# Two-layer trunk with eight experts on one core: order of work at six places of the kernel

## The chip, the cores and the metric

The kernel runs on one core of one Trainium2 chip. The core has TensorE (matrix products, PE in the profile), VectorE (DVE), ScalarE (ACT), GpSimd (POOL) and SyncE (SP), each with a queue of its own that it works through in order; engines wait for each other by semaphores. The metric is the device time of one execution in microseconds (us).

## The reference, cut to what matters

```python
SEQ, D_MODEL = 256, 1024
h = x
# layer 0: one input projection, MLA attention (8 heads) and band attention (8 heads, with a
# learned relative bias), output projection, then a dense SwiGLU
u = rmsnorm(h, g) @ ev_w_in                       # 1024 x 1952
h = h + concat(mla(u), band(u, rel_bias)) @ ev_w_out
h = h + (silu(rmsnorm(h) @ gate) * (rmsnorm(h) @ up)) @ down      # hidden 2752
# layer 1: differential attention, output projection, then top-2-of-8 expert SwiGLU
q, k, v = split(rmsnorm(h) @ od_w_qkv)            # 1024 x 3072
h = h + diff_attention(q, k, v) @ od_w_out
t = rmsnorm(h)
combine = top2_softmax(t @ router)                # 256 x 8
for e in range(8):
    h = h + combine[:, e:e+1] * swiglu(t, gate[e], up[e], down[e])    # hidden 3584
```

## The kernel before

All products are made in three passes to keep float32 accuracy: each weight and each activation is split into a high part (`w_hi`, `xT_hi`, written by ScalarE) and a low rest (`w_lo`, `xT_lo`, written by VectorE), and `product` (L1626) runs hi by hi, hi by low and low by hi. Weights come in units of 1 MB (128 x 2048 floats) in the order of `weight_stream` and, for each expert, `expert_stream` (42 units: gate, up and down of seven chunks of 512 hidden columns, down one chunk behind). A unit goes from memory to `raw` (4, later 7 slots), ScalarE makes `w_hi` and VectorE `w_lo` in a ring of three slots (`SPLIT`), TensorE uses it and counts `unit_used`. So ScalarE can start a unit only when the unit three before it has been used (L625, L860), and `split_to(end)` makes an engine work off the units up to `end` at that place of its queue.

The start: x is transposed by quarters (128 tokens by 512 columns; `norm_turn`), scaled by the gain (`norm_scale`), split (`norm_part` on ScalarE, `norm_low` on VectorE) and used by `project`; the norm's root is applied when the projection is read. The relative bias table is loaded to `rel` by ScalarE's queue (L602), extended by VectorE (L1131), stored to `rel_scratch` by POOL (L2056), waited for, and read back in eight shifted copies (L2060, `bias_rev`); VectorE adds the mask to them (L1190) after router_g and before its part of the second, third and fourth weight units and of the first projection's copy (L1192).

The output projections (`out_projection`) take four units of two k blocks each. The last one goes through `last_unit` (L1644), which works bank by bank (four PSUM banks, tokens by halves of the columns), so that VectorE's residual adds (`add_quarter`, L1049) and TensorE's transposes for the next norm can follow. `add_and_norm` (L1051) is VectorE's order there; ScalarE's is at L771 to L780 (units, table load, norm parts), for the odd layer at L923 to L940.

The dense feed-forward loops over six chunks of 512 (the last of 192): gate and up of chunk j, with the transposes of the hidden product of chunk j-1 into bank 3 behind the gate units (L1848), then the down units of chunk j-1. The last chunk's down unit goes through `last_unit` again.

Routing, ahead of the experts: logits, top 2 (L1437), rank of each token in its expert, gate values (`gates`), and a list of up to three spare items for experts with more than 128 tokens (`spare_items`), all in small VectorE operations; `select` writes 0/1 matrices and TensorE gathers the tokens of two experts at a time. At an expert's end y is read from banks 6 and 7 by ScalarE and VectorE (`outputs`), scattered by TensorE (`scatter`) during the next expert's first units, and added to h (`add_scattered`). After the last expert h goes out in two stores of 128 tokens (L559).

## Time and profile before

| | us |
|---|---|
| median of 3 runs | 1510.41 |
| lowest, highest run | 1499.75, 1512.85 |
| profiled execution, device time | 1512.85 |
| its span, first to last instruction | 1510.7 |

The profile is of one execution. Times in its rows are us from the span's start. A timeline row has the start, the duration, the engine, the line of the kernel, the operation with its tiles, how often it ran in a row, and in brackets how long the engine had been idle and what released it. A queue name with a q (SPq, ACTq) is the issue of a DMA. PEclk is the TensorE clock that was granted, 1.00 being 2.4 GHz and 0.50 being 1.2 GHz.

### The profile page before, as it was taken

To read this page: it belongs to the slowest core of one execution; us is meant where nothing else is said; L and a number is where in the kernel's file an instruction comes from. 1 tells how busy PE (TensorE), PEld (TensorE's weight loads), DVE (VectorE), ACT (ScalarE), POOL (GpSimd) and SP (SyncE) were. 2 spreads that over 40 slices of the span, in tenths; PEclk is the share of its full clock that TensorE was granted. 3 is DMA by queue.
4 is the path that set the end of the run, shared out by engine and by line. 5 is a ranking of instruction groups with operands and counts; after the bars stand their busy time and mean duration, and the time that the engine had idled before them with its cause. 6 is when DMAs were issued, how large, how long until landed. Compare 5 with 4: busy or idle time off the path is not lost.

```text
span 1510.7 us, 17809 instructions
## 1 busy us (share of the span) xinstructions
PE 1448.6 (96%) x6624; PEld 1194.1 (79%) x6624; DVE 1180.3 (78%) x1003; ACT 957.8 (63%) x833; POOL 8.4 (1%) x49
## 2 busy tenths in 40 slices
PE   7989999999987899999999999999999999999997
PEld 5768788886866778888888888888888888888886
DVE  6873554445687688898889889988889988888986
ACT  4562544343464567777777777777777776777774
POOL 2000000000000000000000000000000000000000
PEclk9976999997997899999999999999999999999999
DMA  7400855364532289999999999999999999999992
GB/s 259 162 0 29 307 194 187 111 212 138 170 109 70 98 315 372 375 344 377 379 311 380 371 353 370 378 335 342 372 372 351 377 377 311 371 378 353 367 379 103
DMA packets 181294, 421.51 MB, mean 279 GB/s; under 512 B 9192, under 2 KB 12316, under 8 KB 181212
## 3 DMA queue, kind: packets, MB, share of 16 engines
...
q10 hardware_dynamic: 2496, 0.23, 0.1%
q14 instruction: 25, 0.20, 0.0%
HBM read 419.28 MB, written 1.06 MB: 278 GB/s over the span
## 4 chain that ended last, share of the span: by engine, by line
PE 84%; DVE 10%; ACT 3%; issue 2%; DMA 1%; ACTq 0%; SPq 0%; DVEq 0%
PE ps L1628 25%; PE ps L1630 25%; PE ps L1629 25%; DVE w_lo L1004 2%; PE ps L1959 2%; DVE w_lo L1404 2%; PE ps L1926 1%; DVE h L1525 1%; ACT w_hi L627 1%; PE ps L1711 1%; PE ps L1704 1%; DVE work L1110 1%; DMA raw<-in_ev_w_in_dram 1%; PE ps L1703 1%; PE ps L1641 1%
## 5 line engine op out<-in xcount | busy, mean ns | idle before, releaser
L1404 DVE TENSOR_TENSOR w_lo<-raw,w_hi 128x2048 fp32r<-128x2048 f32 x336 | 768.7, 2290 | 110.3 <-ACT w_hi L861 109.5
L861 ACT ACTIVATE w_hi<-raw 128x2048 fp32r<-128x2048 f32 x336 | 644.2, 1919 | 246.0 <-PE ps L1630 246.0
L1628 PE MATMUL ps<-w_hi,xT_hi 128*128 128x512 f32 (+2 forms) x1312 | 517.9, 395 | 16.3 <-DVE w_lo L999 4.8
L1630 PE MATMUL ps<-w_hi,xT_lo 128*128 128x512 f32 (+2 forms) x1312 | 510.3, 389 | 0.0
L1629 PE MATMUL ps<-w_lo,xT_hi 128*128 128x512 f32 (+2 forms) x1312 | 509.8, 389 | 0.0
L1628 PEld LDWEIGHTS ps<-w_hi,xT_hi 128*128 128x128 f32 x1312 | 248.8, 190 | 68.7 <-issue 11.9
L1630 PEld LDWEIGHTS ps<-w_hi,xT_lo 128*128 128x128 f32 x1312 | 248.6, 189 | 51.4
L1629 PEld LDWEIGHTS ps<-w_lo,xT_hi 128*128 128x128 f32 x1312 | 249.1, 190 | 48.0
L1004 DVE TENSOR_TENSOR w_lo<-raw,w_hi 128x2048 fp32r<-128x2048 f32 (+4 forms) x65 | 138.4, 2138 | 109.8 <-ACT w_hi L627 109.6
L1628 PE MATMUL ps<-w_hi,hT_hi 128*128 128x512 f32 (+1 forms) x548 | 217.8, 397 | 3.0 <-DVE hT_lo L1018 1.9
L1630 PE MATMUL ps<-w_hi,hT_lo 128*128 128x512 f32 (+1 forms) x548 | 215.6, 394 | 0.0
L1629 PE MATMUL ps<-w_lo,hT_hi 128*128 128x512 f32 (+1 forms) x548 | 215.3, 393 | 0.0
L627 ACT ACTIVATE w_hi<-raw 128x2048 fp32r<-128x2048 f32 (+4 forms) x65 | 115.7, 1790 | 130.5 <-PE ps L1630 130.5
L1628 PEld LDWEIGHTS ps<-w_hi,hT_hi 128*128 128x128 f32 (+1 forms) x548 | 104.3, 190 | 27.7 <-issue 3.9
L1630 PEld LDWEIGHTS ps<-w_hi,hT_lo 128*128 128x128 f32 (+1 forms) x548 | 104.4, 191 | 22.0
L1629 PEld LDWEIGHTS ps<-w_lo,hT_hi 128*128 128x128 f32 (+1 forms) x548 | 104.6, 191 | 20.5
L886 ACT ACTIVATE hT_hi<-ps 128x512 fp32r<-128x512 f32 x56 | 33.2, 592 | 9.8 <-PE ps L1959 9.8
L1531 DVE TENSOR_TENSOR hT_lo<-ps,hT_hi 128x512 fp32r<-128x512 f32 x56 | 38.3, 684 | 1.3 <-ACT hT_hi L886 1.3
L1547 DVE TENSOR_TENSOR prod_e<-sil_e,ps 128x512 f32<-128x512 f32 x56 | 38.1, 680 | 0.4 <-PE ps L1630 0.4
L1959 PEld LDWEIGHTS ps<-ident,prod_e 128*128 128x128 f32 x224 | 27.1, 139 | 11.7 <-DVE h L1525 2.9
L1959 PE MATMUL ps<-ident,prod_e 128*128 128x128 f32 x224 | 33.8, 273 | 2.5 <-DVE h L1525 2.5
L1711 PE MATMUL ps<-ident,work 128*128 128x128 f32 x72 | 19.6, 404 | 14.5 <-DVE work L1364 11.4
...
## 6 DMA issues: line engine op xcount, KB each, us to landing
...
```

Source lines behind the costliest of these rows:

```text
L627: ins = act.activation(w_hi[0:r, n % SPLIT, a:a + m], raw[0:r, raw_of(n), a:a + m], ACT.Copy)
L861: act.activation(w_hi[:, (DENSE + q) % SPLIT, :], raw[:, r, :], ACT.Copy).then_inc(hi_ready, 1)
L886: act.activation(hT_hi[:, :, side(m)], blocks(4 + m % 2), ACT.Copy).then_inc(hT_part, 1)
L1004: ins = dve.tensor_tensor(w_lo[0:r, n % SPLIT, a:a + m], raw[0:r, raw_of(n), a:a + m], w_hi[0:r, n % SPLIT, a:a + m].bitcast(F32), ALU.sub ...
L1404: dve.tensor_tensor(w_lo[:, k, :], raw[:, raw_of(DENSE + q), :], w_hi[:, k, :].bitcast(F32), ALU.subtract).then_inc(lo_ready, 1)
L1531: dve.tensor_tensor(hT_lo[:, :, side(m)], blocks(4 + m % 2), hT_hi[:, :, side(m)].bitcast(F32), ALU.subtract).then_inc(hT_ready, 1)
L1547: dve.tensor_tensor(prod_e[:, j % 2, :], sil_e[:, j % 2, :], ps[:, 2 * (j % 2) + 1, :], ALU.mult).then_inc(prod_done, 1)
L1628: pe.matmul(out, x_hi, hi, start=start, stop=False)
L1629: pe.matmul(out, x_hi, lo, start=False, stop=False)
L1630: return pe.matmul(out, x_lo, hi, start=False, stop=stop)
L1711: ins = pe.transpose(ps[:, 2 + head % 2, n * P:(n + 1) * P], s[:, slot, n * P:(n + 1) * P], ident[:, :])
L1959: ins = pe.transpose(ps[:, 4 + j % 2, n * P:(n + 1) * P], prod_e[:, j % 2, n * P:(n + 1) * P], ident[:, :])
```

## The change

Start: weight unit 0 is loaded in two halves with a semaphore each, TensorE begins with its first half (`first_unit`), the order of norm parts and half units on ScalarE and VectorE is changed (`first_low`), the other gains are loaded behind unit 2, and the loads of positions and `rel` are issued behind the fourth norm part, with the extension of `rel` behind `norm_reciprocals(0)` on VectorE. Output projections: units 2 and 3 go through `last_two`, bank by bank over four k blocks, and are both released at its end; VectorE leaves one unit to be split for later (also at the last down unit, where `split_to(last_down + SPLIT)` becomes `split_to(last_down + SPLIT - 1)`) and takes it up inside `add_and_norm`. Feed-forward: the two halves of the last chunk are transposed after the first down unit of chunk 4, the second one into bank `LAST_BANK` (0); VectorE's rest for hT_lo reads the same bank. Routing: `low_tokens(0)` goes behind `select`, the gathers of the high parts come first, ScalarE takes one of the two low copies and loads the table for Silu early; `gates` and the spare items go into the units of expert 0, with the prefix sum over eight counts in three doubling steps instead of seven. Expert's end: the last down unit finishes bank 6 before bank 7, ScalarE and VectorE read them one by one, scatter and adds go by column halves, and h is stored in four parts.

The diff, cut; declarations, the bodies of the small routing functions and VectorE's side of the bank change are left out.

```diff
@@ -508,7 +514,12 @@
     for n in range(DENSE):
-        if n == 2:
+        if n == 0:
+            for c, done in enumerate((first_landed, landed[0])):
+                dst = raw[:, 0, c * UNIT // 2:(c + 1) * UNIT // 2].rearrange("p (k n) -> p k n", k=2)
+                sp.dma_start(dst, w_in[:, 2 * c:2 * c + 2, 0:N]).then_inc(done, 16)
+            continue
+        if n == 3:
@@ -553,11 +564,13 @@
     spare(0)
-    for t in range(TT):
-
-        sp.wait_ge(scatter_read, 4 * (n_over + E) - 2 * (TT - 1 - t))
-        sp.dma_start(out[0, t * P:(t + 1) * P, :], h[:, t, :]).then_inc(stored, 16)
-    sp.wait_ge(stored, 16 * TT)
+    for n in range(4):
...
+        sp.wait_ge(scatter_read, 4 * (n_over + E) - (3 - n))
+        sp.dma_start(out[0, t * P:(t + 1) * P, v], h[:, t, v]).then_inc(stored, 16)
+    sp.wait_ge(stored, 16 * 4)
@@ -598,8 +611,6 @@
     act.dma_start(gain_rows[G_MIX0:G_MIX0 + DC, :], w["ev_norm_mix"][0].rearrange("(k p) -> k p", p=P)).then_inc(mix_landed, 16)
-    act.dma_start(pos_i[:, :], w["positions"][0].rearrange("(t p) -> p t", p=P)).then_inc(pos_landed, 16)
-    act.dma_start(rel[:, 0:2 * B_CLIP + 1], w["ev_b_rel_bias"][0]).then_inc(rel_landed, 16)
@@ -616,11 +627,13 @@
         for n in range(done[0], min(end, DENSE)):
-            act.wait_ge(landed[raw_of(n)], 16 * landings(n))
             if n == 0:
+                act.wait_ge(first_landed, 16)
                 act.activation(w_hi[:, 0, 0:UNIT // 2], raw[:, 0, 0:UNIT // 2], ACT.Copy).then_inc(first_hi, 1)
+                act.wait_ge(landed[0], 16)
...
                 continue
+            act.wait_ge(landed[raw_of(n)], 16 * landings(n))
@@ -703,9 +716,12 @@
     norm_part(0, 0)
+    norm_part(0, 1)
     split_to(1)
-    for f in range(1, 4):
-        norm_part(0, f)
+    norm_part(0, 2)
+    norm_part(0, 3)
+    act.dma_start(pos_i[:, :], w["positions"][0].rearrange("(t p) -> p t", p=P)).then_inc(pos_landed, 16)
+    act.dma_start(rel[:, 0:2 * B_CLIP + 1], w["ev_b_rel_bias"][0]).then_inc(rel_landed, 16)
@@ -786,10 +802,11 @@
                 whole, s = m // P, TT * (j - 1) + t
+                bank = LAST_BANK if j == FCH and t == 1 else 3
...
                 if m % P:
-                    act.activation(hT_hi[0:m % P, whole, t * P:(t + 1) * P], ps[0:m % P, 3, whole * P:(whole + 1) * P], ACT.Copy)
-                act.activation(hT_hi[:, 0:whole, t * P:(t + 1) * P], blocks(3, whole), ACT.Copy).then_inc(ff_hT_hi, 1)
+                    act.activation(hT_hi[0:m % P, whole, t * P:(t + 1) * P], ps[0:m % P, bank, whole * P:(whole + 1) * P], ACT.Copy)
+                act.activation(hT_hi[:, 0:whole, t * P:(t + 1) * P], blocks(bank, whole), ACT.Copy).then_inc(ff_hT_hi, 1)
@@ -876,8 +893,10 @@
     def outputs(i):
-        act.wait_ge(unit_used, i * len(EXPERT) + (DENSE + len(EXPERT)))
+        act.wait_ge(y_psum, i + 1)
         for nn in range(2):
+            if nn:
+                act.wait_ge(unit_used, i * len(EXPERT) + (DENSE + len(EXPERT)))
@@ -940,14 +959,19 @@
     for half in range(2):
-        act.wait_ge(gather_psum, 2 * half + 1)
+        act.wait_ge(gather_psum, half + 1)
...
                        ACT.Copy).then_inc(x_hi_ready, 1)
+    act.wait_ge(gather_psum, 4)
+    bank = FIRST_BANK[3]
+    act.wait_ge(x_lo_ready, 1)
+    act.activation(xT_lo[:, 4:8, :], ps[:, bank:bank + 2, :].rearrange("p b (c n) -> p (b c) n", n=T), ACT.Copy).then_inc(x_lo_ready, 1)
...
     ins.then_inc(gate_exp, 1)
+    act.activation(unread[:, :], eps[:, :], ACT.Silu)
@@ -1058,8 +1083,9 @@
         norm_low(c, 1)
+        norm_low(c, 2)
+        split_to(last + SPLIT)
         norm_scale(k, first, c, 3)
-        norm_low(c, 2)
@@ -1127,24 +1153,24 @@
             ins.then_inc(yT_ready, 1)
-    dve.wait_ge(rel_landed, 16)
-    dve.tensor_copy(rel[:, 2 * B_CLIP + 1:384],
-                    rel[:, 2 * B_CLIP:2 * B_CLIP + 1].to_broadcast([B_HEADS, 383 - 2 * B_CLIP])).then_inc(rel_extended, 1)
...
     norm_low(0, 0)
-    split_to(1)
+    first_low(0, first_hi, first_lo)
     norm_low(0, 1)
+    first_low(1, hi_ready, lo_ready)
...
     norm_reciprocals(0)
+    dve.wait_ge(rel_landed, 16)
+    dve.tensor_copy(rel[:, 2 * B_CLIP + 1:384],
+                    rel[:, 2 * B_CLIP:2 * B_CLIP + 1].to_broadcast([B_HEADS, 383 - 2 * B_CLIP])).then_inc(rel_extended, 1)
@@ -1295,7 +1321,7 @@
     low_y(0, 1)
-    split_to(WIDE_FROM + 2)
+    split_to(WIDE_FROM + 1)
@@ -1404,8 +1431,7 @@
                           ALU.subtract).then_inc(lo_ready, 1)
-    for q in range(SPLIT - 1):
-        split_unit(0, q)
+    split_unit(0, 0)
@@ -1453,7 +1479,6 @@
     link(dve.tensor_scalar(g[:, 9, :, :], g[:, 6, :, :], -FAR, FAR, ALU.mult, ALU.add))
-    low_tokens(0)
@@ -1467,33 +1492,43 @@
-    def spare_items():
...
-        for e in range(1, E):
-            link(dve.tensor_tensor(load8[:, 1, e:e + 1], load8[:, 1, e - 1:e], load8[:, 0, e - 1:e], ALU.add))
...
+    def spare_counts():
...
+    def spare_picks():
...
         link(ins)
...
+    def spare_item(s):
...
+        pick = load8[:, 2 + s:3 + s, :].to_broadcast([P, TT, E])
...
+        dve.tensor_tensor(load8[:, 5 + s, :], load8[:, 2 + s, :], slots_f[:, 0:E], ALU.mult)
...
+    def spare_list():
@@ -1541,6 +1576,17 @@
         for q, (kind, j, u) in enumerate(EXPERT):
+            if routing:
+                if q == 4:
+                    gates()
+                if q == 10:
+                    spare_counts()
+                if q == 16:
+                    spare_picks()
+                if q in (22, 28, 34):
+                    spare_item((q - 22) // 6)
+                if q == 40:
+                    spare_list()
@@ -1566,19 +1612,18 @@
     select(1, 1).then_inc(sel_ready, 1)
-    low_tokens(1)
-    for half in range(2):
-        dve.wait_ge(gather_psum, 2 * half + 2)
-        bank = FIRST_BANK[2 * half + 1]
-        dve.tensor_copy(xT_lo[:, 4 * half:4 * half + 4, :],
-                        ps[:, bank:bank + 2, :].rearrange("p b (c n) -> p (b c) n", n=T)).then_inc(x_lo_ready, 1)
+    for t in range(TT):
+        low_tokens(t)
+    dve.wait_ge(rank_psum, 2)
+    link(dve.tensor_scalar(load8[:, 0, :], ps[:, 7, 0:E], float(P), None, ALU.is_gt))
+    split_unit(0, 1)
+    dve.wait_ge(gather_psum, 3)
+    bank = FIRST_BANK[1]
+    dve.tensor_copy(xT_lo[:, 0:4, :], ps[:, bank:bank + 2, :].rearrange("p b (c n) -> p (b c) n", n=T)).then_inc(x_lo_ready, 1)
     split_unit(0, SPLIT - 1)
-    gates()
-    dve.wait_ge(rank_psum, 2)
-    spare_items()
+    expert(0, 0, False, False, True)
+    expert(1, 0, True, True)
     dve.wait_ge(routed, 1)
-    expert(0, 0, False, False)
-    expert(1, 0, True, True)
@@ -1657,10 +1702,47 @@
             norm_turn(k, f)
+    def last_two(layer, u, hi, lo, hi_2, lo_2):
...
+        for f in range(4):
+            t, half = quarter(f)
...
+            for c in range(4):
+                k = 2 * u + c
+                a, b = (hi, lo) if c < 2 else (hi_2, lo_2)
+                ins = product(ps[:, 4 + TT * t + half, :], xT_hi[:, k, tok], xT_lo[:, k, tok], a[:, c % 2, col], b[:, c % 2, col],
+                              False, c == 3)
+            if f < 3:
+                ins.then_inc(out_psum, 1)
+            else:
+                ins.then_inc(unit_used, 2)
+            if 1 <= f:
+                norm_turn(2 * layer + 1, f - 1)
+        norm_turn(2 * layer + 1, 3)
...
+    def first_unit():
...
+        for c in range(4):
+            if c == 0:
+                pe.wait_ge(first_lo, 1)
+            if c == 2:
+                pe.wait_ge(lo_ready, 1)
+            for t in range(TT):
+                if c == 0:
+                    pe.wait_ge(xT_ready, t + 1)
...
+                ins = product(ps[:, 4 + t, :], xT_hi[:, c, tok], xT_lo[:, c, tok], w_hi[:, 0, col], w_lo[:, 0, col], c == 0, False)
+        ins.then_inc(unit_used, 1)
...
             for u in range(2):
+                if layer == 0 and j == 0 and u == 0:
+                    first_unit()
+                    continue
@@ -1747,8 +1829,8 @@
             hi, lo = split(AT[f"out{layer}", 0, u])
-            if u == DC // 2 - 1:
-                last_unit(2 * layer, 2 * layer + 1, (P, P), xT_hi[:, 2 * u:2 * u + 2, :], xT_lo[:, 2 * u:2 * u + 2, :], hi, lo, True)
+            if u == DC // 2 - 2:
+                last_two(layer, u, hi, lo, *split(AT[f"out{layer}", 0, u + 1]))
@@ -1823,6 +1905,15 @@
     out_projection(0)
+    def turn_hidden(j, t, bank):
...
+        m = cols(j, FF)[1]
+        pe.wait_ge(ff_prod, TT * j + t + 1)
+        for n in range(-(-m // P)):
+            k = min(P, m - n * P)
+            ins = pe.transpose(ps[0:k, bank, n * P:(n + 1) * P], prod[:, t, n * P:n * P + k], ident[:, :])
+        ins.then_inc(ff_turned, 1)
@@ -1845,16 +1936,10 @@
                     ins.then_inc(unit_used, 1)
-                if kind == "gate" and j >= 1:
-
-                    m, s = cols(j - 1, FF)[1], TT * (j - 1) + u
-                    pe.wait_ge(ff_prod, s + 1)
-                    if s >= 1:
-                        pe.wait_ge(ff_hT, s)
...
-                    ins.then_inc(ff_turned, 1)
+                if kind == "gate" and 1 <= j < FCH:
+                    if j >= 2 or u == 1:
+                        pe.wait_ge(ff_hT, TT * (j - 1) + u)
+                    turn_hidden(j - 1, u, 3)
@@ -1872,6 +1957,10 @@
                     ins.then_inc(unit_used, 1)
+                if j == FCH - 1 and k % 4 == 1:
...
+                    turn_hidden(j, 0, 3)
+                    turn_hidden(j, 1, LAST_BANK)
@@ -1929,9 +2018,10 @@
         pe.wait_ge(selT_ready, count)
-        pe.wait_ge(y_lo_ready, 2 * i + 2)
         for n in range(4):
-            t, nn = divmod(n, 2)
+            nn, t = divmod(n, 2)
+            if t == 0:
+                pe.wait_ge(y_lo_ready, 2 * i + nn + 1)
@@ -1971,11 +2061,13 @@
             if kind == "down":
-                for c in range(2):
-                    for nn in range(2):
-                        col = slice(c * D + nn * N, c * D + (nn + 1) * N)
-                        ins = product(ps[:, 6 + nn, :], hT_hi[:, 2 * u + c, side(j)], hT_lo[:, 2 * u + c, side(j)], hi[:, col], lo[:, col],
-                                      j == 0 and u == 0 and c == 0, j == ECH - 1 and u == 1 and c == 1)
+                last = j == ECH - 1 and u == 1
+                for c, nn in ([(0, 0), (1, 0), (0, 1), (1, 1)] if last else [(0, 0), (0, 1), (1, 0), (1, 1)]):
+                    col = slice(c * D + nn * N, c * D + (nn + 1) * N)
+                    ins = product(ps[:, 6 + nn, :], hT_hi[:, 2 * u + c, side(j)], hT_lo[:, 2 * u + c, side(j)], hi[:, col], lo[:, col],
+                                  j == 0 and u == 0 and c == 0, last and c == 1)
+                    if last and (c, nn) == (1, 0):
+                        ins.then_inc(y_psum, 1)
@@ -2017,9 +2109,9 @@
     gather(0, FIRST_BANK[0], T)
+    gather(2, FIRST_BANK[2], T)
...
     gather(1, FIRST_BANK[1], T)
-    gather(2, FIRST_BANK[2], T)
```

## Rows read from the trace of the kernel before

**Rows 1.** The page's first part: busy time, share, instructions

```profile
PE 1448.6 (96%) x6624; PEld 1194.1 (79%) x6624; DVE 1180.3 (78%) x1003; ACT 957.8 (63%) x833; POOL 8.4 (1%) x49
```

**Rows 2.** Windows: PE, PEld, DVE, ACT, POOL busy; PEclk, DMA share, GB/s

```profile
166.00:330.00 164.00, 162.65 (x758) 134.29 (x756) 78.63 (x55) 67.30 (x57) 0.00 (x0) 1.00 0.56 186
1270.00:1390.00 120.00, 119.56 (x543) 98.75 (x542) 107.35 (x62) 88.23 (x60) 0.00 (x0) 1.00 1.00 366
```

**Rows 3.** Timeline (start, duration, engine, line, idle before), start of the kernel

```profile
10.14 1.06 ACT L621 ACTIVATE w_hi<-raw 128x1024 fp32r<-128x1024 f32 x1 [0.57 <-DMA raw<-in_ev_w_in_dram]
...
13.69 0.76 PE L1628 MATMUL ps<-w_hi,xT_hi 128*128 128x512 f32 x1 [4.82 <-DVE w_lo L999]
```

**Rows 4.** Timeline, DMA chain of the bias table

```profile
7.89 0.22 DVE L1131 COPY work<-work 8x127 f32<-8x127 f32 x1 [7.89 <-DMA work<-in_ev_b_rel_bias_dram]
...
15.54 4.27 POOL L2060 DMA_DIRECT2D raw<-rel_scratch  x8 [6.47 <-DMA rel_scratch<-work]
```

**Rows 5.** DMA issues of 0 to 40 us: queue, count, KB each, us to landing

```profile
raw<-rel_scratch POOLq DMA_DIRECT2D x8, 128.0 KB, 4.0
...
pos_i<-in_positions_dram ACTq DMA_DIRECT2D x1, 1.0 KB, 6.7
...
rel_scratch<-work POOLq DMA_DIRECT2D x1, 12.0 KB, 6.8
```

**Rows 6.** One line's instructions: the gain_ff load on POOL, ns each, start

```profile
L2063 POOL DMA_DIRECT2D gain_ff<-in_od_norm_ff_dram x1: 533/533/533, 487.4 to 487.4; - x1
...
DMA to landing us min/median/max: 3.9/3.9/3.9
```

**Rows 7.** Timeline, behind the bias adds

```profile
28.75 2.77 DVE L1190 TENSOR_TENSOR work<-raw,mask 128x256 f32<-128x256 f32 x8
...
33.78 0.50 PE L1628 MATMUL ps<-w_hi,xT_hi 128*128 128x512 f32 x1 [0.41 <-DVE w_lo L1004]
...
39.83 1.00 PE L1687 MATMUL ps<-ident,work 128*128 128x128 f32 x6 [0.32 <-DVE work L1201]
```

**Rows 8.** Timeline, gap in expert 0

```profile
534.07 0.50 PE L1628 MATMUL ps<-w_hi,xT_hi 128*128 128x512 f32 x1 [3.52 <-DVE w_lo L1404]
```

**Rows 9.** Windows as in rows 2: attention, last feed-forward chunk, behind the gap

```profile
85.00:133.00 48.00, 45.32 (x189) 37.82 (x189) 25.02 (x58) 25.58 (x77) 0.00 (x0) 0.56 0.07 23
...
352.00:366.00 14.00, 14.00 (x36) 8.60 (x36) 8.94 (x10) 4.79 (x7) 0.00 (x0) 0.50 0.43 150
...
536.00:538.00 2.00, 2.00 (x6) 1.52 (x6) 2.00 (x2) 0.00 (x0) 0.00 (x0) 0.50 1.02 389
```

**Rows 10.** Timeline, end of the even output projection

```profile
156.62 1.92 ACT L627 ACTIVATE w_hi<-raw 128x2048 fp32r<-128x2048 f32 x1 [3.52 <-PE ps L1630]
158.56 1.28 ACT L643 ACT_TABLE_LOAD   x1
...
161.52 0.66 PE L1641 MATMUL ps<-ident,h 128*128 128x128 f32 x4 [0.91 <-DVE h L1049]
...
165.03 0.47 PE L1628 MATMUL ps<-w_hi,xT_hi 128*128 128x512 f32 x1
```

**Rows 11.** Timeline, last feed-forward chunk

```profile
338.43 0.74 DVE L1320 SCALAR_TENSOR_TENSOR work<-ps,rstd,work 128x192 f32<-128x192 f32 x2
...
350.58 0.79 PE L1628 MATMUL ps<-w_hi,hT_hi 128*128 128x512 f32 x1 [1.04 <-DVE hT_lo L1313]
...
366.41 0.78 PE L1628 MATMUL ps<-w_hi,xT_hi 128*128 128x512 f32 x1
```

**Rows 12.** Timeline, routing

```profile
510.93 0.17 DVE L1435 COPY gate_t<-ps 128x16 f32<-128x16 f32 x1 [1.04 <-PE ps L1907]
...
516.00 2.08 PE L1926 MATMUL ps<-sel,xg_hi 128*128 128x256 f32 x8 [0.64 <-DVE sel L1503]
...
531.52 0.17 DVE L1497 CAST over_i<-over_s 128x4 int32<-128x4 f32 x1
```

**Rows 13.** Timeline, end of the kernel

```profile
1502.60 2.73 DVE L1525 SCALAR_TENSOR_TENSOR h<-ps,comb,h 128x512 f32<-128x512 f32 x4 [0.89 <-PE ps L1937]
```

71 lines of the change are left out of this document (37 added, 34 removed).

## Prediction

> **What bounds the kernel now.** I read the page first [rows 1]: TensorE is busy 1448.6 of 1510.7 us, so 62 us at most are gaps. Then I cut the span into stages [rows 2]. In the experts (busy 119.56 of 120 us, full clock) and in the feed-forward middle (162.65 of 164 us) TensorE has no gap to give back; a change can only pay there if it removes TensorE work, and this one removes none. The time that can move lies in six places: the start, the two ends of the output projections, the last feed-forward chunk, the routing ahead of expert 0, and the end. For each I read the timelines of the engines, since a wait by itself does not tell what is next in the queue. Every engine runs its queue in order, so I look for what stands behind each wait.
>
> The sum is made against the profiled execution (span 1510.7, device time 1512.85, 2.1 us around it). The median of the three runs is 1510.41, and I carry the difference over to it unchanged. The three runs themselves lie 13 us apart, so the kernel can't tell less than about 1% (15 us) from no change.
>
> **Start, first the gain.** Weight unit 0 comes in two halves, and its halves are split around the norm parts. Before, the first product starts at 13.69, released by the second half of w_lo [rows 3]. Now it needs only the first. ScalarE's first half of w_hi starts at 10.14 and takes 1.06 [rows 3]; a norm part now stands ahead of it, but that fits before 10.2, so the half is there at 11.25, and VectorE's half of w_lo, about 1.2, at 12.5. TensorE starts 1.2 us earlier.
>
> **Start, then the loss.** The load of `rel` is issued after the fourth norm part, and VectorE's extension of it now stands behind norm_reciprocals. Behind that lies a chain on POOL that the diff does not touch: store to rel_scratch, wait, eight reads into bias_rev. Before, the extension ran at 7.89, the store took 6.8 us, the reads started at 15.54, the last at 19.3, landing 4.0 us later: 15.2 us from the end of the extension (8.1) to 23.3 [rows 4, 5]. VectorE came to the bias adds at 28.75 and did not wait: 5.4 us of cover. After: the instructions ahead of the extension are the same ones and end at 20.5 in the trace of before and a few tenths later now, 20.9; `rel`, issued near 16.3, lands 4 to 6.7 us later (the 6.7 is that of pos_i beside it [rows 5]), so the extension ends at about 21.5 (20.9 to 22.5). Plus 15.2 is 36.7. The store of before ran beside the weight loads; the one POOL DMA of a quiet time, gain_ff's, took 3.9 [rows 6]. I take the store in the middle, 1.5 us shorter: 35.2 (33.2 with the short store and early extension, 37.7 with the long ones). The bias adds then wait 6.5 us (4.4 to 9.0). Behind them on VectorE stand w_lo of unit 3, which TensorE already waited for at 33.78, w_lo of unit 4, the copy of the first projection and the norms up to TensorE's transposes at 39.83 [rows 7]; all of it moves by the whole wait, and the 1.2 us gained above is swallowed by it. TensorE then stands idle some 8 us. After a gap of 3.5 us at 530 to 534 it ran at the lower level (granted 0.50, 1.2 GHz) until 538 [rows 8, 9]; the 24 products of unit 3 at 0.43 instead of 0.23 us for some 5 us end at 10.3 us after the bias adds where c_normed is ready at 8.1 (39.6, from the end of the bias adds at 31.5): 2.0 us more. Start: +8.5 (5 to 11.5).
>
> The Trainium skill ("DMA: Bandwidth & Descriptors", Anatomy of one DMA) gives a fixed part of about 2.0 us for a DMA of the gpsimd path, against 6.8 us in the row of the store. With 2.0 us for the store and some 2.3 for a read, an estimate from that page, the bias would be there at about 30, the wait 1.3 us, and the sum below 1500 to 1501. That is the second rival.
>
> **Output projections, even layer.** Units 2 and 3 are taken together, bank by bank, and both are given back at the end (unit_used by 2). Gain: VectorE no longer has w_lo of gate unit 1 (2.29) ahead of the residual adds, which cost TensorE 0.91 us at 160.6 [rows 10]. The 48 products (0.2275 each) and two turns from 150.9 end at 162.9, against 163.4. But ScalarE's queue is unchanged: w_hi of gate unit 1, which needs unit 2's slot, then the table load, then the norm parts. Before that w_hi ran at 156.62, under unit 3, and the table load behind it [rows 10]. Now it can't start before 162.9: 1.92 for w_hi, 1.48 for the table load (1.28) and its dummy, 0.63 for the norm part, 0.69 for xT_lo, with handovers 167.8. Gate's first product was at 165.03: +2.8. TensorE has then stood for 3.5 us, the size of the gap in [rows 8], whose 3.5 us at half clock cost 1.7. Even layer: +4.5 (3.7 without the clock but with a 0.9 us wait for w_lo of gate unit 1; 5.5 with a longer low stretch).
>
> **Last feed-forward chunk.** Before, both token halves of the last chunk are turned only after the last down unit of chunk 4 (347.6), with ScalarE, VectorE and bank 3 in series; TensorE starts the last unit at 350.58 and runs it and the transposes at half clock (0.50 over 352 to 366), and the qkv projection starts at 366.41 [rows 9, 11]. VectorE's products were ready at 339.2 [rows 11], so the new turns in mid-down (342) wait for nothing. Then: 347.63 + 0.6 for the moved turns + 18 products (4.1) + turn (0.55) + 6 products (1.4) + turns, the last behind an add of 0.68 and xT_lo of 0.69 = 355.7, at full clock. Gain 10.7, plus 0.4 for the tail at half clock, less 0.7 for w_lo of the second qkv unit, which VectorE reaches at 361.9 when TensorE wants it at 361.2. Feed-forward: -10.4 (-8.5 to -12).
>
> **Odd layer and routing.** Here too ScalarE's w_hi of expert unit 1 waits for the joint release: E = 505.4, w_hi to 507.3, then four copies (0.5 to 0.6) and two squares (1.2) in series: roots at 512.2, logits copied at 512.8 against 510.93. low_tokens(0) no longer stands before the rank (1.28), so the selection ends 1.45 later, not 1.9, and gathers start at 517.45 instead of 516.0 [rows 12]. xT_lo of the first half comes behind w_lo of unit 1: expert 0 starts at 524.05 instead of 522.37. Now the gain: gates and spare items (525.74 to 531.69, 5.9 us, the last of them in [rows 12]) no longer stand before w_lo of unit 3. ScalarE has two table loads and the exponentials first, so w_hi(3) ends at 530.3, w_lo(3) at 532.6, and TensorE goes on at 532.6 instead of 534.07 [rows 8]: 1.5, and I count 1.4. No gap of 3.5 us, so no low stretch: 1.7. Routing: -3.1 (-4.5 to 0).
>
> The some 45 small operations go to seven places in expert 0, about 1 us each. VectorE has 2 us free in each 16.4 us (six w_lo of 2.2, two others of 0.65), and w_lo is ready 1.2 us ahead of its unit, so I charge 0.5 in all (0 to 3).
>
> **Experts' ends.** Seven of eight are covered: the next expert's units run meanwhile, and the releasing order of banks is the same. At the last one y_hi of bank 6 starts six products (1.37 us) earlier, so the last add ends near 1503.8 instead of 1505.3 [rows 13]; four stores of half a row block instead of two, and the last one is 256 KB and does not share with 512 KB: 1.5 + 1.2. End: -2.7 (-1.4 to -3.5).
>
> **Sum.** +8.5 + 4.5 - 10.4 - 3.1 + 0.5 - 2.7 = -2.7 us: span 1508.0, and against the median 1507.7.
>
> **Rivals.** (1) The forecast: two new stalls eat the feed-forward gain; 1507.7. Chance 0.60. (2) The bias is back by 30 us, with both kinds of POOL DMA quicker than any of before; then the start costs 1 instead of 8.5: 1507.7 - 7.5 = 1500.2. For it speaks that the weight loads of the first 20 us are over, against it that even the quiet one of [rows 6] took 3.9 and that eight issues take 4.3 in series. Decides: the landing of the last bias read, before or after 30. Chance 0.20. (3) Neither the start nor the even layer stalls, and both small gains there are kept: -10.4 - 3.1 - 2.7 - 1.2 - 0.9 = 1492. Against it the order of ScalarE's queue. Chance 0.05. (4) The other side: after 8 us of idleness TensorE stays at the lower level through the rest of the input stage, as it did over most of 85 to 133 us [rows 9]; some 30 us of products between 41 and 85 us would cost 15 to 25 us more: 1523 to 1533. It decides if the low stretch lasts past 60 us. Against it: the stretch of [rows 8] ended under unbroken products, and in the input stage they are nearly unbroken. Chance 0.05. (5) The early turns do not do what they say: the last unit still waits, for w_lo or the adds, and the low clock stays; half of the 10.4 is lost: 1512.9. Chance 0.10.
>
> **Chances and range.** Faster by over 1% (below 1495.3): rival 3 and a low draw of rival 2, 0.07. Slower by over 1% (above 1525.5): rival 4 and a little of 5, 0.05. Within: 0.88. The bounds of the terms, all at one end, give 1499.1 (+5 + 3.7 - 12 - 4.5 - 3.5 = -11.3) and 1520.5 (+11.5 + 5.5 - 8.5 + 3 - 1.4 = +10.1); hardly all lean one way, so I cut the top to 1517, and take the bottom to 1495, since rival 2 lies at 1500 before its own terms vary. That holds rivals 1, 2 and 5 but for their outer ends: 8 in 10.
>
> **What would show it.** First product near 12.5; VectorE idle ahead of the bias adds, released by the DMA of bias_rev, 4 to 9 us; TensorE idle from about 32.5 with clock 0.50 behind it. ScalarE's w_hi at the end of the even projections starting with the last product, TensorE idle some 3.5 us. No ScalarE wait of 9 us before the last chunk's hT_hi and clock 1.00 there. No TensorE gap of 3.5 us in expert 0. If the bias read lands under 30 us the first term is wrong; if the w_hi starts earlier than the last product, the second.

## The result and the profile after

| | before | after |
|---|---|---|
| median of 19 runs each | 1508.20 us | 1514.21 us |
| lowest, highest run | 1485.36, 1514.14 | 1496.37, 1517.10 |
| profiled execution, device time | 1512.85 us | 1517.07 us |
| its span | 1510.7 us | 1514.9 us |
| ratio after to before | | 1.0075, 95% interval 1.0044 to 1.0106 |

The changed kernel is slower, by 6.0 us in the medians (0.4%). The ratio of 1.0075 leaves out runs that lie over 1.5% above the fastest of their kernel, the upper eleven of before's 19 and none of after's; with all 19 runs of each the means give 1.0046. The forecast was 2.7 us faster.

The two profiled executions differ by 4.2 us. I set the same points of the work beside each other, from the timelines of TensorE (us from the start):

```
point on TensorE                                     before    after   offset   step
first product of weight unit 0                        13.69    10.67    -3.02
first product of the up-projection (hT)               42.77    51.91    +9.14   start    +9.14
first transpose of the attention output              132.85   141.96    +9.11            -0.03
wait for the first gate's silu                       180.26   194.55   +14.29   even     +5.18
wait for the last gate's silu                        332.59   346.87   +14.28            -0.01
wait for the odd layer's normed q and k              433.98   438.99    +5.01   last FF  -9.27
first gather for expert 0                            516.00   523.18    +7.18   odd      +2.17
first transposes of expert 0                         543.97   546.02    +2.05   routing  -5.13
last transposes of expert 7                         1490.97  1496.52    +5.55   experts  +3.50
end of the span                                     1510.7   1514.9     +4.2    end      -1.35
```

The steps add up to +4.2. The first part of the page after, to be read against [rows 1]: TensorE is busy 3.7 us less, its gaps are 7.9 us longer.

```profile
PE 1444.9 (95%) x6624; PEld 1191.7 (79%) x6624; DVE 1177.8 (78%) x1003; ACT 959.5 (63%) x835; POOL 8.4 (1%) x49
```

Now the stages. The timeline after, start of the kernel, all engines, to be read against [rows 3, 4, 7]:

```profile
8.27 1.04 ACT L632 ACTIVATE w_hi<-raw 128x1024 fp32r<-128x1024 f32 x1
...
10.67 0.47 PE L1673 MATMUL ps<-w_hi,xT_hi 128*128 128x512 f32 x1 [2.32 <-DVE w_lo L1018]
...
21.25 0.22 DVE L1172 COPY work<-work 8x127 f32<-8x127 f32 x1 [2.32 <-DMA work<-in_ev_b_rel_bias_dram]
...
26.09 4.28 POOL L2152 DMA_DIRECT2D raw<-rel_scratch  x8 [3.65 <-DMA rel_scratch<-work]
...
36.87 2.77 DVE L1216 TENSOR_TENSOR work<-raw,mask 128x256 f32<-128x256 f32 x8 [9.14 <-DMA raw<-rel_scratch]
...
41.89 0.80 PE L1673 MATMUL ps<-w_hi,xT_hi 128*128 128x512 f32 x1 [9.58 <-DVE w_lo L1027]
```

The chain is the one foretold: extension at 21.25, store, reads, VectorE 9.14 us idle in front of the bias adds, TensorE 9.58 us idle behind it. The DMA issues of 0 to 40 us after, against [rows 5]: the store is quicker (4.0, was 6.8), the reads slower (6.2, was 4.0).

```profile
raw<-rel_scratch POOLq DMA_DIRECT2D x8, 128.0 KB, 6.2
...
rel_scratch<-work POOLq DMA_DIRECT2D x1, 12.0 KB, 4.0
```

The end of the even output projection after, timeline, against [rows 10]: ScalarE's w_hi is the last product's follower, the table load stands behind it, and gate starts 3.54 us late.

```profile
172.12 1.91 ACT L640 ACTIVATE w_hi<-raw 128x2048 fp32r<-128x2048 f32 x1 [9.95 <-PE ps L1675]
174.05 1.28 ACT L656 ACT_TABLE_LOAD   x1
...
177.01 0.76 PE L1673 MATMUL ps<-w_hi,xT_hi 128*128 128x512 f32 x1 [3.54 <-DVE xT_lo L1041]
```

Windows after (busy us of PE, PEld, DVE, ACT, POOL, then PEclk, DMA share, GB/s), behind the two new gaps, in the last feed-forward chunk and in expert 0, against [rows 9]. Behind both gaps TensorE runs at 1.2 GHz (granted 0.50, the first window already holds some full clock); in the last chunk, where before it had 0.50 over 352 to 366, it now has 1.00; and expert 0 has no gap left.

```profile
42.00:46.00 4.00, 4.00 (x11) 3.16 (x12) 3.04 (x4) 1.78 (x2) 0.00 (x0) 0.57 0.73 225
...
177.00:181.00 4.00, 3.99 (x10) 3.13 (x11) 2.64 (x5) 2.59 (x7) 0.00 (x0) 0.50 0.81 299
...
352.00:366.00 14.00, 14.00 (x62) 10.58 (x61) 7.64 (x12) 7.15 (x10) 0.00 (x0) 1.00 0.72 243
530.00:546.00 16.00, 15.93 (x70) 12.81 (x69) 11.67 (x12) 13.33 (x12) 0.00 (x0) 1.00 0.79 282
```

The qkv projection of after starts at 371.30, 4.89 us later than in [rows 11] instead of 14.3. What the forecast had not reckoned with lies in the experts. From expert to expert the first transposes are 120.4 or 120.5 us apart, with a pair's gathers 123.8 to 124.2, and at one place more: from expert 3 to expert 4, where the loop over the middle pairs jumps back, before takes 124.96 and after 128.07. The timelines of VectorE and then of TensorE at that place, before:

```profile
1008.44 1.23 DVE L1510 CAST xT_lo<-ps 128x1024 fp32r<-128x1024 f32 x1 [0.89 <-PE ps L1926]
1010.34 2.29 DVE L1404 TENSOR_TENSOR w_lo<-raw,w_hi 128x2048 fp32r<-128x2048 f32 x1 [0.67 <-ACT w_hi L861]
...
1014.75 0.49 PE L1628 MATMUL ps<-w_hi,xT_hi 128*128 128x512 f32 x1 [0.87 <-issue]
```

and after, VectorE and then TensorE:

```profile
1010.53 1.22 DVE L1545 CAST xT_lo<-ps 128x1024 fp32r<-128x1024 f32 x1 [0.89 <-PE ps L2015]
1016.14 4.49 DVE L1431 TENSOR_TENSOR w_lo<-raw,w_hi 128x2048 fp32r<-128x2048 f32 x2 [4.38 <-ACT w_hi L878]
...
1018.49 0.79 PE L1673 MATMUL ps<-w_hi,xT_hi 128*128 128x512 f32 x1 [2.52 <-DVE w_lo L1431]
```

The row of after names ScalarE's w_hi as what VectorE waited for. But that w_hi started at 1010.50 and took 1.91 us, so it was ready at 1012.4, and VectorE began only at 1016.14; in before it began as soon as w_hi was there (1010.31 and 1010.34). VectorE stood 3.7 us longer. The DMA queues of the 15 us around it, before (1003 to 1018) and after (1007 to 1022):

```profile
q1 hardware_dynamic: 2027, 4.17, 82.6%
q8 instruction: 2, 0.03, 0.8%
```

```profile
q1 hardware_dynamic: 1415, 2.82, 56.1%
q8 instruction: 2, 0.03, 0.8%
q14 instruction: 4, 0.03, 0.6%
```

After has four instruction loads of 8 KB on queue 14, at 1008.8, 1014.1, 1016.6 and 1019.0, and before none between 903 and 1257 us.

### The profile page after: what moved, and what is told of

Same layout as the page of the kernel before. It is cut to its first block, busy times and chain, and to the rows that moved or that the text cites. A ratio compares the mean times of both kernels' runs of the same rounds, so it can differ in the third digit from the quotient of the medians.

```text
span 1514.9 us, 17822 instructions
## 1 busy us (share of the span) xinstructions
PE 1444.9 (95%) x6624; PEld 1191.7 (79%) x6624; DVE 1177.8 (78%) x1003; ACT 959.5 (63%) x835; POOL 8.4 (1%) x49
## 4 chain that ended last, share of the span: by engine, by line
PE 84%; DVE 9%; ACT 3%; issue 2%; DMA 1%; POOL 0%; DVEq 0%; ACTq 0%
PE ps L1673 25%; PE ps L1675 25%; PE ps L1674 25%; PE ps L2049 2%; DVE w_lo L1027 2%; DVE w_lo L1431 2%; PE ps L1793 1%; PE ps L2015 1%; DVE h L1560 1%; ACT w_hi L878 1%; ACT w_hi L640 1%; PE ps L1786 1%; DVE work L1136 1%; PE ps L1808 1%; PE ps L1809 1%
## 5 line engine op out<-in xcount | busy, mean ns | idle before, releaser
L1793 PE MATMUL ps<-ident,work 128*128 128x128 f32 x72 | 19.6, 403 | 14.3 <-DVE work L1391 11.2
```

Of the source, the lines that this page charges most:

```text
L1793: ins = pe.transpose(ps[:, 2 + head % 2, n * P:(n + 1) * P], s[:, slot, n * P:(n + 1) * P], ident[:, :])
```

## The experiments

Each experiment has one profiled execution; f1 has four timed runs, f2 to f4 have six each, beside eleven of before on the same chip. Lines of diffs are cut with "...". Times between two points below are those of the table above.

**e1, e2, e3: the start.** Three edits of the changed kernel. e1 loads early:

```diff
+            act.dma_start(pos_i[:, :], ...
+            act.dma_start(rel[:, 0:2 * B_CLIP + 1], ...
             def load_rows():
...
             norm_part(0, 3)
-            act.dma_start(pos_i[:, :], ...
-            act.dma_start(rel[:, 0:2 * B_CLIP + 1], ...
```

> The changed kernel with one edit: the loads of rel and positions are issued at the start again, as before the change; VectorE's extension of rel stays behind norm_reciprocals. In the changed kernel VectorE waited 2.32 us for rel (until 21.25) and 9.14 us for the bias reads (until 36.87). Theory 1 (the bias-table chain behind the extension, 15 us long, sets the start): the wait for rel goes, the extension is 2.3 us earlier, the bias adds start at 34.5 after a wait of 6.8, and the first uq product comes at 49.6 instead of 51.91. Rival (the late load alone is the cause, not the place of the extension): the bias adds do not wait and uq comes near 42. Rival 2 (the new order of the first unit costs the time, not the bias): uq stays at 51.9.

Bias adds of e1, timeline: at 34.05 behind 6.87 us, and the up-projection at 49.90. This is theory 1 (34.5, 6.8 and 49.6); both rivals fall.

```profile
34.05 2.77 DVE L1216 TENSOR_TENSOR work<-raw,mask 128x256 f32<-128x256 f32 x8 [6.87 <-DMA raw<-rel_scratch]
```

e2 also moves the extension:

```diff
             first_low(1, hi_ready, lo_ready)
+            dve.wait_ge(rel_landed, 16)
+            dve.tensor_copy(rel[:, 2 * B_CLIP + 1:384], ...
```

> The changed kernel with the early load and the extension of rel behind VectorE's second half of w_lo of unit 0, near 12 us instead of 21.25. Theory 1: with 15 us from extension to landing the bias is there at 27.3, VectorE comes to it near 27.7 and does not wait; the first product stays near 10.7 and uq comes at 41 to 42, 10 to 11 us earlier than in the changed kernel (51.91) and 1 to 2 us earlier than before (42.77). Rival 2 (the new order of the first unit costs): no more than 2 us come back.

The up-projection came at 45.42, not at 41 to 42. VectorE did not wait for the bias, but for another load in front of it. Timelines of e2, VectorE and TensorE:

```profile
29.15 0.36 DVE L1206 TENSOR_TENSOR lamv<-lamv 128x64 f32<-128x64 f32 x2 [5.21 <-DMA router<-in_od_router_dram]
...
30.36 2.77 DVE L1216 TENSOR_TENSOR work<-raw,mask 128x256 f32<-128x256 f32 x8
...
35.38 0.50 PE L1673 MATMUL ps<-w_hi,xT_hi 128*128 128x512 f32 x1 [3.60 <-DVE w_lo L1027]
```

In its DMA issues the router rows take 6.7 us to land; in after they took 3.7:

```profile
router<-in_od_router_dram ACTq DMA_DIRECT2D x1, 32.0 KB, 6.7
```

The eight bias reads (issued 19.83 to 24.1) now fall on the small row loads (issued 18.3 to 23.1). The wait moved from one load to the next in VectorE's queue. e3 leaves both loads late and moves the consumer:

```diff
-            dve.wait_ge(bias_landed, 16 * B_HEADS)
-            for head in range(B_HEADS): ...
             project("in", 0, u0, EVEN_IN, [0])
...
             project("in", 0, u0, EVEN_IN, range(1, UP_AFTER))
+            dve.wait_ge(bias_landed, 16 * B_HEADS)
+            for head in range(B_HEADS): ...
```

> The changed kernel with the eight bias adds moved behind the projections of chunk 1 on VectorE, where it stood idle for 3.78 us ahead of 60.71; the late load and the late extension stay. Theory 1 (VectorE's wait matters only for what is queued behind it): the bias still lands near 36.9, nobody waits for it, w_lo of unit 3 starts at 27.7 instead of 39.6, TensorE has no gap ahead of unit 3 and no half clock behind it; uq comes at 39.5 to 41. The 2.8 us of adds cost nothing at their new place. Rival (contention or a late landing elsewhere): uq later than 43. Rival 2: stays at 51.9.

Timelines of e3: w_lo of unit 3 at 27.43, the bias adds at 45.15 without a wait, the up-projection at 40.65, 11.26 us earlier than after and 2.12 earlier than before. So the whole start loss came from what stood behind the wait in VectorE's queue, and no load had to be moved.

```profile
27.43 2.29 DVE L1027 TENSOR_TENSOR w_lo<-raw,w_hi 128x2048 fp32r<-128x2048 f32 x1
...
45.15 2.77 DVE L1236 TENSOR_TENSOR work<-raw,mask 128x256 f32<-128x256 f32 x8
```

**e4: ScalarE's order at the even output projection.**

```diff
-            split_to(WIDE_FROM + SPLIT - 1)
+            split_to(WIDE_FROM + SPLIT - 2)
             load_root_table()
             norm_part(6, 0)
             norm_square(1, 0)
             norm_part(6, 1)
+            split_to(WIDE_FROM + SPLIT - 1)
```

> The changed kernel with one edit on ScalarE's queue at the end of the even output projection: w_hi of gate unit 1, which needs the slot of out-projection unit 2, stands behind the table load and two norm parts instead of ahead of them; the joint release of units 2 and 3 stays. In the changed kernel the first gate product came at 177.01 behind a gap of 3.54 us, 2.9 us later against its neighbours than before, and 2.3 more went to the half clock behind it. Theory 2 (ScalarE's queue order is the cause): the gap is under 1.5 us, gate starts near 173.5 to 174, no stretch at half clock of more than 3 us, and the point of unit 20 us later comes 5 us earlier (189.5 instead of 194.55). Rival (taking the two units together costs by itself): gate starts no earlier than 176. Middle case: the gap goes and the half clock stays, 2.9 us back.

Timelines of e4, ScalarE and TensorE: w_hi at 170.03 behind two norm parts; gate starts at 169.00 right behind the last transposes. From the attention's transposes to the silu wait it takes 48.29 us instead of 52.59 (before 47.41): 4.3 of 5.2 back, and the clock stays at 1.00 from 170 to 188. A new wait of 2.16 us for w_lo of the moved unit has come in.

```profile
170.03 1.90 ACT L640 ACTIVATE w_hi<-raw 128x2048 fp32r<-128x2048 f32 x1
...
176.87 0.50 PE L1674 MATMUL ps<-w_hi,xT_hi 128*128 128x512 f32 x1 [2.16 <-DVE w_lo L1028]
```

**f1: the two units one by one.** The changed kernel with `last_unit` in place of `last_two` in both layers and the old places of `split_to` around `add_and_norm`:

```diff
-                    if u == DC // 2 - 2:
-                        last_two(layer, u, hi, lo, *split(...
+                    if u == DC // 2 - 1:
+                        last_unit(2 * layer, 2 * layer + 1, (P, P), ...
```

> The changed kernel with the last two units of both output projections taken one by one again (VectorE's place of the next w_lo in the residual adds as before the change). Theory 2 (the joint release of the slots is a loss in both layers): in the even layer the turn of the attention output to the gate unit 20 us later takes 47.4 us again instead of 52.6 (5.2 back), in the odd layer first out-projection product to first gather 35 to 36 us instead of 38.2 (2 to 3 back), in all 7 to 8 us less than the changed kernel. Rival (the odd layer gains by it, as the change means): only 5 back. Start, feed-forward and the back edge between expert 3 and 4 (128.05) stay as in the changed kernel.

Even layer 46.87 us instead of 52.59. Odd layer, first out-projection product to first gather: 474.99 to 508.24 = 33.2 instead of 38.2. So the joint release costs in both layers, and the rival falls. The sizes, 5.7 and 4.9 us, are those of one pair of executions. Over all executions the even stretch took 50.6 to 52.6 us in the ten kernels with the joint release and ScalarE's order of after, and 46.8 to 47.4 in the nine without it: 3.2 to 5.8 us. TensorE's gap is 3.5 us in all ten; what runs ahead of it and the clock behind it differ. In the odd layer the other kernels with the new routing and no joint release, e6, f3 and f4, took 34.8 us and not 33.2, against 38.1 to 38.7: at least 3.2 us, still more than the 2 to 3 expected. Median 1501.53, ratio to before 0.996 (0.9929 to 0.999): the rest of the change, with the start loss still in it, is a little faster than before.

**e5, f2: the feed-forward part alone**, on the kernel before:

```diff
+                bank = LAST_BANK if j == FCH and t == 1 else 3
...
-                        if kind == "gate" and j >= 1:
+                        if kind == "gate" and 1 <= j < FCH:
...
+                        if j == FCH - 1 and k % 4 == 1:
+                            turn_hidden(j, 0, 3)
+                            turn_hidden(j, 1, LAST_BANK)
```

> The kernel before with only the feed-forward part of the change (the last chunk's two turns inside the last down of chunk 4, two banks). Theory (the wait for the turn chain and the half clock behind it are what was gained): from the start of the down products of chunk 4 to the start of the qkv projection 20.4 us instead of 29.7 before (336.69 to 366.41), clock 1.00 there, nothing else moves; the span falls by 9 to 9.5. Rival (half of it lost, the clock stays low or w_lo of the last unit is late): 24 to 25 us there. The time of the experts' back edge (first turn of expert 3 to first turn of expert 4) stays at 124.96, as before.

From the last gate's silu wait to the wait for the odd layer's normed q and k (332.59 to 433.98 in the table; the expectations call this stretch chunk 4 to the qkv chunks) it takes 91.45 us; before took 101.39. So 9.9 us, a little more than the theory's 9 to 9.5, with clock 1.00. Its span, 1498.2, is 12.5 shorter than that of the profile before, more than the edit: other stages differ too (below). A single run of before beside it took 1499.87 us where e5 took 1500.37, so single totals decide nothing here. The back edge takes 125.25 (expected 124.96).

> The kernel before with only the feed-forward part, timed. The profiles of kernels with the old last chunk show two cases there: 101.4 us from chunk 4 to the second qkv chunk with clock 0.50 after the wait (before, and the one with only the routing part), and 95.1 us with clock 1.00 (the one with only the experts' ends); with the new chunk it was 91.5. Theory 4 (TensorE's clock after that wait differs from execution to execution, so the profiled one of before shows more to gain than the median holds): the median gains 4 to 8 us, ratio 0.995 to 0.997. Rival (the half clock is there in nearly every execution): 9 to 10 us, ratio 0.9935.

Median 1500.19 against 1507.56 of before on that chip: 7.4 us, ratio 0.9946, 95% interval 0.9919 to 0.9973. The median's gain lies in theory 4's 4 to 8 us, the ratio between the two theories, and its interval holds both: the timing does not decide. The profiles show what the theory rests on: the old last chunk took 101.39, 101.35 and 101.32 us in three executions (before, e6, g4), and 95.13 in a fourth (e7). Windows of e7 over the same stretch as [rows 9], clock 1.00 with the old order:

```profile
352.00:366.00 14.00, 13.37 (x65) 10.66 (x66) 11.84 (x17) 8.40 (x11) 0.00 (x0) 1.00 0.41 142
```

So 9.9 us of gain in an execution of the first kind and 3.7 in one of the second; the new order took 91.4 to 92.2 us in all 16 profiled executions that have it. Within these 16 there is a second, small split: 91.4 or 91.5 in the five with the old place of `split_to` at the last down unit (e5, f1 to f4), 92.1 or 92.2 in the eleven that leave one unit for later as after does. Leaving the unit for later costs 0.7 us there.

**e6, e7: routing alone, experts' ends alone**, on the kernel before.

```diff
+                    if routing:
+                        if q == 4:
+                            gates()
...
-            gates()
-            spare_items()
...
```

> The kernel before with only the routing part (selection order, spare items inside expert 0, gates there). Theory: router products to first turn of expert 0 take 36.8 us before and 33 us here (-3.9, of which 1.7 is the half clock that goes); the seven places in expert 0 cost TensorE nothing, its seven turns of expert 0 stay 16.79 us apart. On the 3.1 us that the changed kernel loses once between expert 3 and expert 4, where the loop over expert pairs jumps back (first turn to first turn 128.05 instead of 124.96): if what stands ahead of the loop on VectorE decides (the routing operations moved there change where the loop's code lies), it is 128 here and 125 in the run with only the experts' ends; if the added waits and the new order inside the loop decide, it is 125 here and 128 there.

Router products to first transposes of expert 0: 504.60 to 535.94 = 31.34 us, before 36.78. It is 5.4 us and not 3.9. The 3.9 came from the changed kernel, which took 32.84 us; f1, which has the new routing without the joint release, took 31.57, so the joint release had taken some of it. The transposes of expert 0 are 16.8 us apart: its seven groups of small operations cost TensorE nothing. The back edge takes 126.74 and is neither 128 nor 125. Timelines of e6, VectorE and TensorE: the same stall as in after, without the half clock behind it.

```profile
1006.10 4.49 DVE L1409 TENSOR_TENSOR w_lo<-raw,w_hi 128x2048 fp32r<-128x2048 f32 x2 [4.45 <-ACT w_hi L861]
...
1008.45 0.50 PE L1651 MATMUL ps<-w_hi,xT_hi 128*128 128x512 f32 x1 [2.59 <-DVE w_lo L1409]
```

```diff
-                t, nn = divmod(n, 2)
+                nn, t = divmod(n, 2)
...
-                act.wait_ge(unit_used, i * len(EXPERT) + (DENSE + len(EXPERT)))
+                act.wait_ge(y_psum, i + 1)
...
```

> The kernel before with only the experts' ends (y by banks with a semaphore of its own, scatter and stores in column order, four stores). Theory of the end: last turns to the end of the span 18.4 us instead of 19.7, the last add 1.5 us earlier behind the last product and the stores none. Rival (my forecast): 17.0. On the loop's back edge, expert 3 to 4: 128 here if code inside the loop decides, 125 if the code ahead of it does. The six other boundaries stay within 0.3 us of before.

Back edge 124.93, as before: not the changed order inside the loop. e6 has the stall, and its edit leaves VectorE's code inside the loop as in before; it changes only what stands ahead of it. Last transposes to the end of the span 18.07 us, before 19.73.

**e8: no loops.**

```diff
-            with dve.Fori(1, PAIRS - 1) as p:
+            for p in range(1, PAIRS - 1):
...
-            with sp.Fori(1, E) as i:
+            for i in range(1, E):
```

> The changed kernel with the loop over expert pairs (and SyncE's over experts) written out on every engine, so that no engine jumps back; all work and its order are unchanged. Theory 3 (the 4.3 us more at expert 3 to 4 than at expert 1 to 2, 128.05 against 123.79, is a fetch of instructions after the backward jump; VectorE stands idle for 4.38 us there although ScalarE's w_hi is ready): 123.8 there, span 4 to 4.5 us shorter. Rival a (weights arriving late there, the DMA queue being full): stays at 128. Rival b (fetches cost elsewhere as well once the code is longer): other boundaries grow.

123.94 us from expert 3 to 4 instead of 128.07: the whole excess goes, and no other boundary grows by more than 0.2. Theory 3 holds, rivals a and b fall.

**g1, g2: which engine.** The same edit for VectorE alone, and for all the others.

> The changed kernel with only VectorE's loop over expert pairs written out; the others still jump back. Theory 3a (it is VectorE's backward jump: it stood idle 4.4 us there with its operand ready, in the changed kernel and in the one with only the routing part, not in the others): expert 3 to 4 takes 124 to 125 us instead of 128.07. Rival: another engine's jump is late too, 126 or more.

> The reverse: the loops of TensorE, ScalarE and SyncE written out, VectorE's kept. Theory 3a: VectorE still stands idle some 4 us after its jump, expert 3 to 4 takes 127 to 128 us. Rival: the cost needs several engines to fetch at once, 125 or less.

g1 takes 125.13, g2 128.57. The 3 us that after has over before are VectorE's jump. The 1.2 us that g1 still has over 123.9, as before has them, go only with the other engines' loops too: TensorE's gap there is 1.02 us in g1 and 0.87 in before, with nothing that the profile shows as its cause ("issue"). g1's timeline of VectorE has no stall, and no load on queue 14 around it; g2 has them.

```profile
1012.32 2.29 DVE L1431 TENSOR_TENSOR w_lo<-raw,w_hi 128x2048 fp32r<-128x2048 f32 x1 [0.67 <-ACT w_hi L878]
```

All 20 profiled kernels agree. Eleven have the new routing and VectorE's loop: VectorE stands 4.25 to 4.50 us at the jump, with the four loads. Five have the old routing and the loop, and four have VectorE's loop written out: none of these nine has the stall or the four loads.

**g3 to g6: does the place of the code decide?**

```diff
             chain = [0]
+            for _ in range(128):
+                dve.nop()
```

> The changed kernel with 128 nops at the head of VectorE's queue, which has nothing to do for its first microseconds; the loop's code is the same and lies 128 instructions later. Theory 3b (where the loop's code lies decides how long the jump back waits): expert 3 to 4 differs from 128.07 by over 1 us. Rival (the changed order of work at that place costs it, whatever the code's place): 128.0 to 128.2.

> The kernel before with the same 128 nops. Theory 3b: expert 3 to 4 may become 126 to 128 us although nothing else is changed; the rival: 124.9 to 125.3 as in every kernel whose code ahead of the loop was that of before. It is also one more sample of the last feed-forward chunk of before: chunk 4 to the second qkv chunk 101.4 us with clock 0.50 after the wait, or 95.1 with clock 1.00.

> The changed kernel with 32 nops at the head of VectorE's queue. With 128 nops the gap of TensorE behind VectorE's jump was the same as in the changed kernel (2.59 against 2.52 us), only the clock behind it was 1.00 instead of 0.50. A shift by 128 may be a whole number of the pieces in which the code is loaded. Theory 3b (place of the code within such a piece): with 32 or with 64 nops the gap behind the jump goes, to 1 us or less. Rival (what VectorE ran in expert 0 and 1, not the place, decides): 2.4 to 2.7 us in both.

> The same with 64 nops. Theory 3b: in one of the two the gap behind the jump is 1 us or less, expert 3 to 4 near 125. Rival: 2.4 to 2.7 us in both, expert 3 to 4 126.7 (clock 1.00) or 128.1 (clock 0.50).

g3 took 126.73, which looks like theory 3b, but its timeline shows TensorE's gap unchanged and only the clock behind it at 1.00:

```profile
1013.24 0.50 PE L1676 MATMUL ps<-w_hi,xT_hi 128*128 128x512 f32 x1 [2.59 <-DVE w_lo L1434]
```

With 32 and 64 the gap was 2.52 and 2.50 (128.03 and 128.22 us), and in g4 before kept its 125.12. That would speak for the rival, but the traces show that the place of the code was not tested. They have no rows for nops, and the loads on queue 14 come behind the same instruction of VectorE, to within one, in after, g3, g5 and g6 (the 187th, 283rd, 573rd and 961st of its rows, for example), and in g4 as in before. Nops that had moved the code by 32 or 64 instructions would have been expected to move these points.

The Trainium skill ("Advanced Engine Details and Errata", ISA Cache) gives an engine other than TensorE an instruction cache of only two lines of 256 instructions; by it a loop that lay in them whole could come to lie across a third. That the code is loaded again behind the jump agrees with it; the 8 KB of each load on queue 14 is half of the 16 KB that the page gives for a line. No run here shows whether the place of the loop or what ran ahead of it is the reason. That stays open.

**f3, f4: what paid, together.** f3 is the changed kernel with the edits of f1, e3 and e8.

> What paid, together: the changed kernel with the output projections' last units one by one again, the bias adds behind the projections of chunk 1, and the loop over expert pairs written out. By the local figures against the kernel before: start -2.1, feed-forward -3.7 to -9.9, routing -5.2, back edge -1.2, experts' ends -1.3, sum -13.5 to -19.7: ratio 0.987 to 0.991. Rival (the terms are not independent, a gain at the start is taken back by the clock in the scores): a third of it is lost, ratio 0.994.

Median 1487.93 against 1507.56: 19.6 us, ratio 0.9866 (0.9838 to 0.9894). The theory, at its upper end. The span is 1488.0; the first part of its page:

```profile
PE 1435.2 (96%) x6624; PEld 1185.2 (80%) x6624; DVE 1177.9 (79%) x1003; ACT 959.7 (64%) x835; POOL 8.4 (1%) x49
```

f4 is f3 with the early load and extension of e2; it moves the work that waits for the row loads behind w_lo of units 3 and 4 and stores by column half (the last two shown):

```diff
+            split_to(AT["in", 0, 1] + SPLIT + 1)
             dve.wait_ge(rows_landed, 16 * n_rows)
...
-            for n in range(4):
+            for nn in range(2):
...
-                sp.dma_start(out[0, t * P:(t + 1) * P, v], h[:, t, v]).then_inc(stored, 16)
+                sp.dma_start(out[0].rearrange("(t p) d -> p t d", p=P)[:, :, v], h[:, :, v]).then_inc(stored, 16)
```

> The combined kernel with two edits more. Start: rel and positions loaded at the start again, its extension near 12 us, and the sums of the lambda rows, the gains and router_g, which wait for the small row loads, behind w_lo of units 3 and 4. With the extension early and the bias adds ahead of w_lo the row loads (router 6.7 us instead of 3.7 beside the eight bias reads) became the wait, 5.2 us; here nothing of TensorE's weights is queued behind them. Expected: unit 2 starts at 24.8 instead of 26.4 and uq at 39 instead of 40.65. Rival (a next wait comes in): uq at 40.6 or later. End: two stores of 512 KB, each both token halves of one column half, instead of four of 256 KB: the last issue is 0.3 us earlier, its size double; 0 +- 0.5 us.

The up-projection starts at 39.69 (f3 40.48, expected 39), and the last transposes are 16.89 us from the end (f3 17.89). Median 1488.84, ratio 0.9869 (0.9843 to 0.9895): no difference from f3 that these runs can tell. The gain at the end is not one either: that stretch took from 16.25 to 18.52 us in the profiles with four stores.

## Why the prediction failed

**Start: right in mechanism, +9.14 for +8.5, and the number in part by luck.** Extension, chain on POOL, wait, the queue behind it and the half clock came as worked out. Two terms were off and nearly cancelled. The landing of the reads was taken from [rows 5] at 4.0 and took 6.2, so the bias adds came at 36.87 instead of 35.2, 1.7 later. From there to the up-projection it took 15.04 us where before had 14.02 (28.75 to 42.77): the term for the half clock measured 1.0 and not 2.0. The extension's time came out by luck too: `rel` was issued at 13.99 and not near 16.3, and landed about 7 us later, not 4 to 6.7. The first product came at 10.67 instead of 12.5: ScalarE's first half of w_hi started at 8.27, since in [rows 3] it had waited for its load and in [rows 4] VectorE's norm work stood behind the wait for `rel`; I had kept both waits. As foretold this gain was swallowed. Rival 2 needed the bias by 30; it landed at 36.9. So the 2.0 us that the Trainium skill ("DMA: Bandwidth & Descriptors", Anatomy of one DMA) gives as a DMA's fixed part did not size this chain; the rows do, with 4.0 and 6.2.

**Even output projection: right, +5.18 for +4.5.** ScalarE's queue was read rightly (2.87 for the order, 2.3 for the clock, where 2.8 and 1.7 were worked out); e4 and f1 confirm the cause. The size is that of this execution: among the ten kernels with this order the stretch took up to 2.0 us less.

**Last feed-forward chunk: right in this execution, -9.27 for -10.4, but its size is not one number.** The 10.4 counted a half clock that is there in three of four profiled executions of the old order. I took one execution for the kernel. The 0.7 us that I had subtracted for w_lo of the second qkv unit are there (91.4 against 92.1). The two cases may be part of why the medians differ by 6.0 and the profiles by 4.2; how often each occurs in the timed runs no run shows.

**Odd layer and routing: right in the sum, -2.96 for -3.1**, from +2.17 and -5.13. From the wait for q and k to the first transposes of expert 0, e6 with the routing alone takes 6.6 us less than before (432.52 to 535.94 against 433.98 to 543.97), and after 3.0 less: both the gain of the routing and the cost of the joint release, 3.6 here, were taken too small.

**Experts: wrong, +3.50 for +0.5 (0 to 3).** This is the failed step. I priced the small operations in expert 0, which cost nothing, and took the other seven experts to run as before, since [rows 2] shows no gaps there. But 120 us windows hide one place. The loop's back edge costs 3.1 more: 1.8 of wait, because VectorE stands while its code is loaded again, and 1.3 of half clock behind it (g3 and e6, with the same gap and full clock behind it, take 126.73 and 126.74). The other 0.4 lies at the other boundaries, 0.3 of it from expert 5 to 6. No row was read at the jump, though before itself shows 1.2 us there.

**End: half right, -1.35 for -2.7.** From the last expert product (ScalarE's y_hi right behind it starts at 1499.79 and 1505.34) to the end of the adds (1505.33 and 1509.31) the time fell from 5.5 to 4.0 us, the 1.5 foretold. The 1.2 for smaller stores did not come: four issues on SyncE take 3.05 us in series against 1.68 for two, and after the last add the span runs on for 5.6 us, before 5.4. The -1.35 is that of one pair: from the last transposes to the end the five kernels with the stores of before took 19.0 to 20.0 us and the fourteen with four stores 16.25 to 18.52, 1.8 us less in the mean. The last adds of after, timeline, against [rows 13]:

```profile
1506.59 2.72 DVE L1560 SCALAR_TENSOR_TENSOR h<-ps,comb,h 128x512 f32<-128x512 f32 x4
```

**Sum and chances.** The forecast's span was 1508.0 and it was 1514.9: 6.9 too low, of which the experts are 3.0, the end 1.35, the feed-forward 1.1, the even layer 0.7, the start 0.6, the odd layer and routing 0.1. The steps of the start and of the odd layer and routing lie near their forecasts by terms that offset each other. The range of 1495 to 1517 held the time. "Within 1%" at 0.88 held too, but the likeliest sign was wrong, and none of the rivals was the back edge. Rival 5's 1512.9 lies near the measured time by luck: the early turns did what they were to do.
